# Two of the six modulation groups move from TensorE and the weight ring to VectorE, in the second block's dense stage

## The reference

```
block(x, c):
    sh1, sc1, g1, sh2, sc2, g2 = split(silu(c) @ w_mod + b_mod, 6)     # "modulation": 6 x 1024 columns
    x = x + g1 * [norm](mixer(rms_norm(x) * (1 + sc1) + sh1))
    x = x + g2 * [norm](moe(rms_norm(x) * (1 + sc2) + sh2))
```

## Time and profile before

| | |
|---|---|
| median of three runs | 1979.17 us |
| the profiled execution, its own time | 1975.73 us |
| its span, first to last instruction | 1973.9 us |
| TensorE busy | 1793.9 us (91%) |
| VectorE busy | 522.7 us (26%) |
| ScalarE busy | 394.9 us (20%) |
| GpSimd busy | 51.0 us (3%) |
| mean DMA rate | 318 GB/s |
| mean granted TensorE clock | 0.978 |

### The profile page before, as it was taken

How to read it: one execution, slowest core, us unless ns; L and a number is a source line. 1 busy time by engine, 2 the same in 40 slices (tenths; PEclk the granted TensorE clock), 3 DMA queues, 4 the chain that set the end, 5 groups by cost and what they waited for, 6 DMA issues and landing times.

```text
span 1973.9 us, 27226 instructions
## 1 busy us (share of the span) xinstructions
PE 1793.9 (91%) x10815; PEld 988.7 (50%) x10816; DVE 522.7 (26%) x1208; ACT 394.9 (20%) x912; POOL 51.0 (3%) x109
## 2 busy tenths in 40 slices
PE   7999999986867999899999999998897999989987
PEld 4766777754544667678743333333333333333332
DVE  4685331132212240342541111111111111111112
ACT  3343552021101220433111110011110111101111
POOL 0040000000000010100010000000000000000000
PEclk9999999998978999999999999999999999999999
DMA  9979315439999752423466999999999799999996
GB/s 398 409 268 394 138 65 216 168 150 394 422 411 413 303 109 93 84 59 102 167 261 257 428 427 428 427 429 427 429 427 428 292 427 428 428 428 428 427 428 284
DMA packets 57691, 626.81 MB, mean 318 GB/s; under 512 B 7360, under 2 KB 11456, under 8 KB 13472
## 3 DMA queue, kind: packets, MB, share of 16 engines
q1 hardware_dynamic: 55744, 620.09, 76.2%
q0 software_dynamic: 1584, 4.33, 2.1%
q10 hardware_dynamic: 272, 1.05, 0.1%
HBM read 624.39 MB, written 1.05 MB: 317 GB/s over the span
## 4 chain that ended last, share of the span: by engine, by line
PE 59%; DMA 32%; DVE 3%; issue 3%; ACT 2%; DVEq 0%; SPq 0%; ACTq 0%
PE ps L500 57%; DMA ring<-in_w_gu_dram 27%; DMA ring<-in_moe_w_gate_dram 4%; PE ps L667 2%; DMA ring<-in_w_dn_dram 1%; ACT arena L1549 1%; ACT arena L1720 1%; DMA hN<-in_x_dram 1%; DVE stat L2114 0%; DVE arena L2131 0%; SPq L525 0%; PE ps L663 0%; DVEq L1992 0%; DVE hN L2007 0%; DVE rstd L1963 0%
## 5 line engine op out<-in xcount | busy, mean ns | idle before, releaser
L500 PE MATMUL ps<-ring,arena 128*64 128x512 f32 (+2 forms) x4416 | 734.9, 553 | 97.7 <-DMA ring<-in_w_gu_dram 48.5
L500 PEld LDWEIGHTS ps<-ring,arena 128*64 128x64 f32 (+1 forms) x4416 | 242.6, 128 | 534.6 <-issue 418.0
L500 PE MATMUL ps<-arena 128*32 128x256 f32 (+13 forms) x2434 | 382.6, 452 | 38.3 <-ACT arena L1549 15.5
L500 PEld LDWEIGHTS ps<-arena 128*64 128x64 f32 (+8 forms) x2434 | 171.2, 146 | 225.3 <-issue 157.7
L500 PE MATMUL ps<-hT,ring 128*128 128x256 f32 (+1 forms) x960 | 236.1, 401 | 5.0 <-DVE hT L2040 2.0
L500 PEld LDWEIGHTS ps<-hT,ring 128*128 128x128 f32 x960 | 179.4, 191 | 60.5 <-issue 35.6
L1549 ACT ACTIVATE arena<-ps 128x512 f32<-128x512 f32 (+4 forms) x191 | 104.7, 571 | 312.2 <-PE ps L500 178.2
L2385 DVE TENSOR_SCALAR arena<-ps 128x512 f32<-128x512 f32 (+1 forms) x34 | 23.0, 676 | 509.5 <-PE ps L500 509.5
L1815 ACT ACTIVATE arena<-ps,mod,gain 128x128 f32<-128x128 f32 x176 | 66.1, 458 | 422.4 <-PE ps L500 422.4
L1827 ACT ACTIVATE arena<-arena 128x512 f32<-128x512 f32 (+1 forms) x44 | 25.3, 575 | 567.4 <-DVE arena L2385 375.9
L500 PEld LDWEIGHTS ps<-arena,hN 128*128 128x128 f32 x896 | 104.6, 193 | 32.4 <-issue 18.0
(11 more groups left out here) (306 smaller groups left out, 908.3 us busy)
## 6 DMA issues: line engine op xcount, KB each, us to landing
ring<-in_w_gu_dram SPq DMA_DIRECT2D x96, 2048.0 KB, 25.5
ring<-in_w_dn_dram SPq DMA_DIRECT2D x64, 2048.0 KB, 21.4
arena<-in_w_gu_dram SPq DMA_DIRECT2D x32, 2048.0 KB, 27.3
ring<-dense_dram SPq DMA_DIRECT2D x56, 1024.0 KB, 8.9
ring<-in_moe_w_up_dram SPq DMA_DIRECT2D x16, 2048.0 KB, 15.7
ring<-in_moe_w_down_dram SPq DMA_DIRECT2D x16, 2048.0 KB, 15.0
ring<-in_ada_w_dram SPq DMA_DIRECT2D x24, 1024.0 KB, 18.0
ring<-in_w_mod_dram SPq DMA_DIRECT2D x24, 1024.0 KB, 7.8
```

Of the source, the lines that this page charges most:

```text
L500: ins = nc.tensor.matmul(*a, start=start, stop=stop, **k)
```

## The change

1. The chunks of groups 4 and 5 leave the ring's list (16 chunks), and TensorE no longer computes them: the list ends at `MODS = 24`. `turn_modulation(3)` moves behind the compressed keys. Ring positions behind them shift by 16.
2. The same 4096 columns of `w_mod_2` are given to the kernel transposed, as 32 tiles of 128 columns x 1024 rows (512 KB each, one row of 4 KB for each partition).
3. TensorE writes silu(c_2) as a row that is repeated on all partitions, by 8 matmuls behind the first projection of the second dense stage, and ScalarE copies it to `late_row`.
4. GpSimd loads the tiles: six at once, into three new places in the arena, half of `hN`, and two places in `o2`; each further one when VectorE has used the tile six before it. Its first bias loads wait for "r1" in place of ("moe1", 3), and the tiles stand between the two sets of bias loads.
5. VectorE multiplies each tile with the row and sums it to one column of `mod2`, behind rope and ahead of attention 2. Then it adds the bias and makes three gains that it made in the first block before. The mark ("shift", 2), for which TensorE's router row waits, moves behind this.

```
+MODS = 24
+LATE = 32
+    out["late_dram"] = np.ascontiguousarray(I["w_mod_2"][:, 2048:].T).reshape(LATE, P, D)
-        mod_chunks(24, 8)
...
-            if c % 2 == 0:
-                mod_chunks(32 + 2 * c, 4)
...
+        late = [carve(15872 + 1024 * j, 1024) for j in range(3)] + [hN[:, 1, :], carve(at2 - 2048, 1024), carve(at2 - 1024, 1024)]
+        late_row = hN[:, 0, :]
...
# SyncE, before the spare pieces of moe1
-            sp.wait_ge(filled, nth(filled, ("mod columns", 5)))
+            sp.wait_ge(filled, nth(filled, ("branch", 3)))
# GpSimd
-            g.wait_ge(filled, nth(filled, ("moe1", 3)))
+            g.wait_ge(filled, nth(filled, "r1"))
             for tt in range(TT):
+                if tt == 1:
+                    for i in range(LATE):
+                        if i >= 6:
+                            g.wait_ge(late_used, i - 5)
+                        g.dma_start(late[i % 6], A["late"][i]).then_inc(late_in[i % 6], 16)
                 if tt == 1:
                     g.wait_ge(filled, nth(filled, ("S", 2, 3)))
# TensorE, key compression
-            modulations(3)
             ssm_outputs(13)
...
-            modulations(3)
             ssm_outputs(14)
...
-            modulations(2)
-            turn_modulation(4)
+            turn_modulation(3)
# TensorE, branch products
-                if c % 2 == 0:
-                    modulations(4)
...
-            turn_modulation(5)
...
-                if c == 2:
-                    pe.wait_ge(emptied, nth(emptied, ("mod columns", 5)))
# TensorE, second dense stage, behind kvb2
+            for k in range(KD):
+                last = mm(ps[:, 4 + k // 4, (k % 4) * P:(k % 4 + 1) * P], csil[:, KD + k:KD + k + 1].broadcast_to([P, P]), ident,
+                          start=True, stop=True)
+            last.then_inc(filled, mark(filled, "late row"))
# ScalarE, behind the two copies of kvb2
+            act_.wait_ge(filled, nth(filled, "late row"))
+            for h in range(2):
+                last = copy(late_row[:, h * 512:(h + 1) * 512], ps[:, 4 + h, :])
+            last.then_inc(emptied, mark(emptied, "late row"))
# VectorE, behind rope
+            v.wait_ge(emptied, nth(emptied, "late row"))
+            for i in range(LATE):
+                w = late[i % 6]
+                v.wait_ge(late_in[i % 6], 16 * (i // 6 + 1))
+                V.tensor_tensor_reduce(w, w, late_row, 1.0, 0.0, ALU.mult, ALU.add, mod2[:, 16 + i, 0:1]).then_inc(late_used, 1)
+            v.drain()
+            step(tt_(mod2[:, 16:48, 0], mod2[:, 16:48, 0], cols[:, 1, 16:48], ALU.add))
+            tt_(gain[:, 4, :], mod2[:, 16:24, 0], cols[:, 1, 56:64], ALU.mult)
+            stt(gain[:, 5, :], mod2[:, 32:40, 0], 1.0, cols[:, 1, 64:72], ALU.add, ALU.mult)
+            tt_(gain[:, 0, :], mod2[:, 40:48, 0], cols[:, 1, 72:80], ALU.mult).then_inc(madeV, mark(madeV, ("shift", 2)))
+            v.drain()
             attention(2, units2)
```

More of the change, by code:

```diff
@@ L367, in mod_chunks @@
         def mod_chunks(f, n):
-            for i in range(f, min(f + n, 40)):
+            for i in range(f, min(f + n, MODS)):
                 mod_chunk(1 + i // 8, i % 8)
@@ L402, in program @@
         front2_at = moe1_at + 3 * E
+        assert n_front1 == moe1_at
         n1 = len(chunks)
@@ L439, in weights @@
             i = index[key]
-            later = 0 if i < n1 else moe1_at // RING + sum(1 for x in range(front2_at, i + 1) if x % RING == i % RING)
-            eng.wait_ge(full[i % RING], 16 * (later or i // RING + 1))
+            uses = sum(1 for x in range(i + 1) if x % RING == i % RING and (x < n1 or x >= front2_at))
+            eng.wait_ge(full[i % RING], 16 * uses)
             return slot_ap(i, chunks[i if i < n1 else i - front2_at + n1][2])
@@ L455, in program @@
         biasb_in = sem("expert_biases_in")
+        late_in = [sem(f"late_modulation_in{j}") for j in range(6)]
+        late_used = sem("late_modulation_used")
         xin = sem("x_in")
@@ L688, in modulation @@
                 w = weights(pe, ("mod", g, k))
-                if k == 0 and g == 5:
-                    pe.wait_ge(madeV, nth(madeV, ("constant", 1)))
-                elif k == 0 and g >= 1:
+                if k == 0 and g >= 1:
                     pe.wait_ge(emptied, nth(emptied, ("mod rows", g - 1)))
                 for m in range(4):
-                    last = mm(ps[32 * m:32 * m + 32, 7 if g == 5 else 3, :], cpad[:, k, :], w[:, m, :], start=k == 0, stop=k == KD - 1)
+                    last = mm(ps[32 * m:32 * m + 32, 3, :], cpad[:, k, :], w[:, m, :], start=k == 0, stop=k == KD - 1)
                 if k == KD - 1:
@@ L713, in modulations @@
             def modulations(n):
-                for i in range(mods_done[0], min(mods_done[0] + n, 40)):
+                for i in range(mods_done[0], min(mods_done[0] + n, MODS)):
                     g, k = 1 + i // 8, i % 8
-                    if k == 2 and 2 <= g <= 4:
+                    if k == 2 and 2 <= g <= 3:
                         turn_modulation(g - 1)
@@ L2156, in attention @@
                         maxima(n, i + 2, units[i + 2])
-            v.wait_ge(emptied, nth(emptied, ("mod columns", 4)))
+            v.wait_ge(emptied, nth(emptied, ("mod columns", 3)))
             tt_(mod1[:, 16:48], mod1[:, 16:48], cols[:, 0, 16:48], ALU.add)
-            step(tt_(mod2[:, 0:32, :], mod2[:, 0:32, :], B(cols[:, 1, 0:32], 2), ALU.add))
+            step(tt_(mod2[:, 0:16, :], mod2[:, 0:16, :], B(cols[:, 1, 0:16], 2), ALU.add))
             V.memset(rtok[:, :], 1.0).then_inc(madeV, mark(madeV, ("shift", 1)))
@@ L2211, in _ @@
             clear_tables(1)
-            v.wait_ge(emptied, nth(emptied, ("mod columns", 5)))
-            step(tt_(mod2[:, 32:48, :], mod2[:, 32:48, :], B(cols[:, 1, 32:48], 2), ALU.add))
-            stt(gain[:, 5, :], mod2[:, 32:40, 0], 1.0, cols[:, 1, 64:72], ALU.add, ALU.mult)
-            tt_(gain[:, 0, :], mod2[:, 40:48, 0], cols[:, 1, 72:80], ALU.mult)
             for c in range(4):
```

17 lines of the change are left out of this document (5 added, 12 removed).

## The result

The changed kernel takes 1966.65 us (median of 5 runs, 1960.88 to 1972.04) against 1978.96 (5 runs, 1977.05 to 1982.54): ratio 0.9936, 95% interval 0.9919 to 0.9953. The forecast was 1966.2. The profiled execution took 1960.88 (span 1959.3), 14.85 less than that of before; the forecast difference was 13.0.

The account below looks back on a forecast made before the run. TensorE was taken to bound the stretch ahead of moe1 and the second dense stage, transfers the expert stages. Group 4 -7.2, group 5 -7.7, row +1.9, rest 0: -13.0, giving 1966.2 us on the median; range 1963 to 1975.

Parts of the forecast that it names:

- Group 4, -7.2: Ahead of attention in the first block: without 8 chunks, attention starts at 176.5 in place of 183.68; bounds -5.5 and -8.5.
- Rival (e): First block: covers that were missed eat half of group 4's gain; -9.5 in all, 1970 us; chance 6%.
- rival (d): The 14.9 us won ahead of moe1 don't pass through it, since its transfers don't start earlier; 1981 us; chance 4%.
- Group 5, -7.7: First block: two blocks at 3.57 us and 0.5 for the turn leave TensorE; bounds -7.1 and -7.9.
- The ring, 0: The freed 16 MB in the ring gain nothing, as TensorE, not the transfer, ended the waits; bounds 0 and -1.
- Products, 1.35 us each: VectorE between rope and attention 2's first maximum: 32 products with sum, 43 us alone, fit; bounds 1.2 and 2.3 + 0.1.
- Rival (b): VectorE's product with sum runs at the scan's speed, 2.4 us each: +7.6 in all, 1987 us; chance 5%.
- Loads, 1.67 us a tile: GpSimd's queue, shared with SyncE's projections: the loads set the products' pace, 26 tiles in 43.4 us.
- Rival (c): Transfers of GpSimd's queue don't overlap: 4.3 us a tile, 58 late, +45, 2024 us; chance 3%.
- The store's stops, 4.4 us: GpSimd's descriptor store holds 14 tiles, so two stops fall among the 26, 4.4 us together.
- Room, 4 us; 0 in the sum: VectorE's late work ends at 797.9, 4 us ahead of attention 2's first maximum at 801.9, so it costs 0.
- Rival (a): Tiles come too slowly (1.9 to 2.2 us each, or longer stops); attention 2 starts 2 to 10 late; 1968 to 1976; 18%.

Follow-up runs that it names:

- fill: Changed kernel with TensorE's matmuls for both groups put back at their old places on resident data, without loads or group 5's turn: 1978.65 us, ratio 0.9995.
- part5: Changed kernel with only group 5 computed late and group 4 back at its old place (16 tiles, 16 products): 1977.44 us, ratio 0.9983.
- part4: Changed kernel with only group 4 computed late and group 5 back in the first block: 1980.37 us, ratio 1.0000.
- again2: The changed kernel unchanged, run once more on the chip of the next three kernels: 1966.41 us, ratio 0.9929.
- more16: Changed kernel with sixteen more VectorE products behind the 32, on resident data, sums not used: 1978.85 us (10 runs).
- best: Changed kernel with the silu(c_2) row made without TensorE and eight idle products ahead of each of two waits in attention 2: 1962.66 us, ratio 0.9913.
- again: The changed kernel unchanged, run once more as a common base: 1963.39 us, ratio 0.9912.
- store1024: Changed kernel with half the store of descriptors for GpSimd's queue (1024 in place of 2048): 1973.25 us, one run.

## Why the prediction was right, step by step

- **What bounds it.** Right, and shown by fill: 16.5 us of TensorE's time given back at the old places ((a), (c), (d)), with no transfers, undo the whole gain.
- **Group 4, -7.2.** Measured 7.19 (part5 against after) and 7.1 (after against before, less the clock). The forecast called the row at 170.44 in the earlier trace rows `modulations(2)`; it is the first two chunks of `modulations(3)`, and the price of a chunk is the same. Rival (e) is dead with this, and rival (d) with the first transfer wait of moe1, 19.2 us earlier. The wait that appears for VectorE is 1.19 us; 1.2 had been laid out (171.9 to 173.1).
- **Group 5, -7.7.** Measured 7.98 (before against after; part4 against after has 7.97). Mis-sized by 0.3, and fill says where: with both blocks and no turn its (c) is 7.54 above the changed kernel's. So a block costs 3.77 us and not 3.57, and the turn 0.44 where 0.5 was taken. In the rows, the 32 matmuls ahead of the first block take 7.11 us to its start, 0.2 more than the 6.92 of each 32 in the unbroken row of the changed kernel. Not foreseen at all: 1.64 us more in the stretch (d), where the clock stayed up in most kernels without group 5 (not in again2 and more16, so it is no rule).
- **The ring, 0.** Right within what can be seen: fill has the changed kernel's ring, with products and row, and its ratio to before is 0.9995; its (c) of 84.98 against 85.42 is the turn that it leaves out. A few us either way couldn't be seen.
- **The row, +1.9.** 1.78 in the trace, 1.8 by best against again.
- **Products, 1.35 us each.** 1.15. The operation writes its product at the plain speed, and the sum's own row (0.08) overlaps the next product. Rival (b) is dead by a factor of two.
- **Loads, 1.67 us a tile.** 1.69, right by more luck than the step deserves: the engines moved 407 to 423 GB/s in that stretch (733 to 769, by 4 us), all queues together, but the share that SyncE took came in bursts and not as an even 23%. VectorE waited five times, 0.4 to 3.4 us, each time 4 to 10 us behind the issue of a ring chunk (at 735, 749 and 762) and never else; that the chunk made the wait is read from this order alone. Rival (c) is dead: the shortest landing of a tile was 3.8 us, the median 8.6, and still one came every 1.69.
- **The store's stops, 4.4 us.** Wrong: no stop came, and this is the one step whose mechanism failed. The 1.6 us of start and end in each stop had no row behind it either. I had counted the pieces issued since the last stop; what fills the store is the pieces under way. With six places these are 768 of 2048. What I had read of the length of a stop, until the last one issued has landed, is right (store1024).
- **Room, 4 us; 0 in the sum.** Right in the sum. The window was 57.6 us (57.5 forecast); the work took 49.0 of it and not 53.5, about the 4.4 of the stops, so 8.6 us were left. The cheaper products gave nothing, since the tiles set the pace. more16 shows that beyond the room (f) grows by every us (8.8 measured, 9.6 asked for). Rival (a) would have needed 1.69 + 8.6 / 26 = 2.0 us a tile.
- **The sum.** Between the two profiled spans lie 14.6 us: 7.1 (group 4) + 8.0 (group 5) - 1.8 (row), 13.3 where 13.0 were forecast; + 1.7 (clock, a) + 1.6 (clock, d) - 1.7 (clock, in the first projection of f) and, unforeseen and not caused by any step, + 2.9 (e), - 1.7 (g; the scores with 1.44 and 2.08 us, a step of the clock again), - 1.6 (i), + 0.1. So the steps carry the result, and 1.3 us of it is the luck of these two executions. Such steps, and moe1 with 274.4 to 279.2 in nine profiles of kernels with the same work up to there, make up most of what differs between profiles of the same code; why moe1 varies stays open.

## What to carry to other kernels

Look for the engine that is idle while the bounding one is at 100%, and move there what has a late due time: the price of a group on TensorE is read from two rows, and the room for it on the other engine is one idle time in front of one instruction. Count a queue's limit by what can be under way at once, not by what has been issued. And when a kernel with half of a change doesn't gain half, compare the stages that neither half touches before believing in an interaction: here 4 to 6 us were missing, most of a group's own price, and they lay in the expert stages.

## What the hardware showed beyond that

- One code's runs differ by up to 11 us. A part of it are steps of 1.65 to 1.7 us, each one stretch of some 3 us in which TensorE has 1.2 in place of 2.4 GHz (granted clock 0.50 from 676 to 679 and from 789 to 791 in the changed kernel), behind idle times of 1.6 and 2.2 us. The same idle times stand in other profiles without the step.
- A VectorE product with sum of 128x1024 float32 is 1.22 us, start to start 1.15 with the sum read out.
- A wait `<-issue` of 2.0 to 3.8 us at a loop's entry or turn appears or goes with edits outside the loop. The kernels that have it at the entry of moe2 take 2 to 4 us more for that stage, beside a gain of 14.
- With half the descriptor store the issues of 16 loads took 33.6 us in place of 19.4, and (g) was 6 to 9 us longer (one run).
